# Retention's chunk loop reordered one chunk deeper on four engines

## The chip, the cores and the metric

One of the eight cores of a Trainium2 chip runs the kernel. The metric is the device time of one execution in microseconds (us). Five engines of the core work at once, each through its own list of instructions in order: TensorE (PE in the profile, its weight loads PEld), VectorE (DVE), ScalarE (ACT), GpSimd (POOL) and SyncE (SP), which here only starts DMA transfers. They wait for each other by semaphores.

## The reference

The reference is one layer of a hybrid decoder, for a prompt of 1024 tokens and for 64 new tokens (8 sequences of 8). What the change touches is the retention half of the mixing sub-layer. The prompt is cut into 8 chunks of 128 tokens, and a state S per head is carried from chunk to chunk. Per chunk:

```
inner = einsum('bihd,bjhd->bhij', q, k) * decay[None]
o = (einsum('bhij,bjhe->bihe', inner, v)
     + einsum('bihd,bhde->bihe', q, S) * cross_decay[None, :, :, None])
S_new = S * exp(C * log_g) + einsum('bjhd,bjhe,jh->bhde', k, v, k_decay)
```

Each head's output of 64 values is then normalized and gated:

```
mu = mean(ro); var = mean(square(ro - mu))
ro = (ro - mu) * rsqrt(var + GN_EPS) * g_ret
ro = ro * silu(rg)
```

The new tokens go through the same formula with a state of their own for each sequence. Beside retention the layer has a dilated window attention, an output projection and a SwiGLU feed-forward part.

## The kernel before

The program runs in stages, each a block that every engine enters and leaves together: the input projection (to about 372 us of the span), retention (about 376 to 477), the prompt's attention, the new tokens' attention, and the output projection with the feed-forward part. The change is in the retention block alone. The projection has already rotated, scaled and gated the operands and left them in DRAM; `zr[t]` holds chunk t's q, k, v and gate, 1 MB each, loaded by SP.

Chunk t (0 to 7; `SAMPLE` = 8 stands for the new tokens) takes these steps, each a small function in its engine's part:

- PE `turn(t)` (L845) transposes q and k into `qk_ps`; ACT `evacuate(t)` (L716, L717) copies them to `qT` and `kT`, which have two places each.
- PE `inner(t)` (L856) multiplies them into `in_ps`; DVE `scores(t)` (L741) multiplies that with the mask into `inT`. Both exist once, so `scores(t)` waits for the output of chunk t-1, which reads `inT`, and `inner(t+1)` waits for `scores(t)`.
- PE `update(t)` (L864) computes the chunk's share of the state into `su_ps`; DVE `carry(t+1)` (L759, L761) adds it into `S`, which has two places.
- PE `output(t)` (L873 with the state, L876 with `inT` and v) writes `o_ps`, which has two places.
- DVE `centre(t)` (L774 to L780) sums `o_ps`, takes the mean off and writes `oc`; ACT `square(t)` (L724) squares it; DVE `variance(t)` (L786, L788) sums the squares; POOL `late(t)` raises the variance to the power -0.5 (L692) and scales `oc` into `on` (L696); DVE `finish(t)` (L795) multiplies with the gate into `mixr`, which has two places and which SP stores to DRAM.

`oc` and `on` exist once. The order of the work is the order in which these functions are called on each engine. On DVE a pass of the loop is scores(t), carry(t+1), variance(t-1), finish(t-1), centre(t); on PE inner(t), update(t), turn(t+1), output(t); on ACT evacuate(t+1), square(t); on POOL late(t). In the pass of t = 2 DVE also builds a small table (`build_rows`, L574). After the loop stands the tail for the new tokens: PE multiplies a bias table (`sample_products`, L593), then 64 small products with the loaded states and 16 with `inT` (L894, L897), then the new states (L906); DVE does scores, the last state, a large masked copy `vm` (L645), centre(SAMPLE), the states' sums (L824) and two table copies (L581), with which the block ends.

Of the kernel before, what the change touches and what calls it, by code (L numbers as in the profile page):

```python
# [28 lines left out]
ACT = mybir.ActivationFunctionType  # L29
# [3 lines left out]
HD, NH, NPAIR = 64, 8, 4  # L33
# [7 lines left out]
PT = SEQ // 128  # L41
TT = PT + 1
# [97 lines left out]
def spread(ap, shape):  # L140

    return ap.unsqueeze(2).broadcast_to(shape)
# [385 lines left out]
class DistanceTables:  # L528
# [4 lines left out]
    rows = staticmethod(lambda g: 66 if g == 2 else 99)  # L533
# [26 lines left out]
    def finish(self, sp):  # L560
        sp.wait_ge(self.bias_landed, 16 * NH)
# [37 lines left out]
def retention(nc, A, z, mix, ident, ret, state_p, state_s, tab, bias_p, bias_s, kept_on, stored, ahead):  # L599


    with ExitStack() as ctx:
        sb = lambda n, s, d=F32: ctx.enter_context(nc.sbuf_tensor(n, s, d))
# [7 lines left out]
        inT = sb("inT", [128, 2, NPAIR, 128])  # L611
        S = sb("S", [128, 2, NPAIR, 128])
        kd = sb("kd", [NS, NH, HD])
        oc, sq, on = (sb(n, [128, NH, HD]) for n in ("oc", "sq", "on"))
        stat, mhalf = sb("stat2", [128, TT, 5, NH]), sb("mhalf2", [128, NH])
        mixr, S_out, S_last = kept_on
        S_in = sb("S_in", [128, DEC_B, NPAIR, 128])
# [17 lines left out]
        def head(t, a, h, n=1):  # L635
            return zr[t][0:tile_rows(t), a, h:h + n, :].rearrange("t h d -> t (h d)")
# [11 lines left out]
        with nc.Block() as block:  # L648
# [32 lines left out]
            @block.gpsimd  # L681
            def _(pool):
                pool.memset(mhalf[:, :], -0.5).then_inc(cleared, 1)
                pool.memset(S[:, :, :, :], 0.0).then_inc(cleared, 1)
                pool.memset(qdm[:, :, :], 0.0).then_inc(cleared, 1)
                pool.memset(S_in[:, :, :, :], 0.0).then_inc(cleared, 1)
                pool.wait_ge(cleared, 1)

                def late(t):
                    rows = tile_rows(t)  # L690
                    pool.wait_ge(var_ready, t + 1)
                    pool.tensor_tensor(stat[0:rows, t, 4, :], stat[0:rows, t, 3, :], mhalf[0:rows, :], ALU.pow).then_inc(rstd_ready, 1)  # L692
                    pool.wait_ge(rstd_ready, t + 1)
                    if t:
                        pool.wait_ge(mix_ready, t)
                    pool.tensor_tensor(on[0:rows], oc[0:rows], spread(stat[0:rows, t, 4, :], [rows, NH, HD]),  # L696
                                       ALU.mult).then_inc(on_ready, 1)

                for t in range(PT):
                    late(t)  # L700
                    if t == 3:
                        pool.wait_ge(landed[SAMPLE], 16)
                        pool.tensor_tensor(kd[:, :, :], zr[SAMPLE][0:NS, 1], spread(last_s[:, :], [NS, NH, HD]),
                                           ALU.mult).then_inc(kd_ready, 1)
                    if t == 5:
                        one_sequence(pool, slice(DEC_B // 2 + 1, DEC_B))
                late(SAMPLE)

            @block.scalar
            def _(act):  # L710
                def evacuate(t):
                    rows = tile_rows(t)
                    act.wait_ge(qk_turned, t + 1)
                    if t >= 2:
                        act.wait_ge(o_done, t - 1)
                    act.copy(qT[:, t % 2, :, 0:rows], qk_ps[0][:, :, 0:rows])  # L716
                    act.copy(kT[:, t % 2, :, 0:rows], qk_ps[1][:, :, 0:rows]).then_inc(qkT_ready, 1)  # L717

                def square(t):
                    rows = tile_rows(t)  # L720
                    act.wait_ge(oc_ready, t + 1)
                    if t:
                        act.wait_ge(square_sum_ready, t)
                    act.activation(sq[0:rows], oc[0:rows], ACT.Square).then_inc(sq_ready, 1)  # L724

                evacuate(0)
                for t in range(PT):
                    evacuate(t + 1)
                    square(t)
                square(SAMPLE)  # L730

            @block.vector
            def _(dve):
                def scores(t):
                    rows = tile_rows(t)
                    dve.wait_ge(inner_done, t + 1)
                    if t:
                        dve.wait_ge(o_done, t)
                    own = mask if t < PT else mask_s
                    for r in range(2):  # L740
                        x = dve.tensor_tensor(inT[0:rows, r, :, 0:rows], in_ps[r][0:rows, :, 0:rows],  # L741
                                              own[:, :].unsqueeze(1).broadcast_to([rows, NPAIR, rows]), ALU.mult)
                    x.then_inc(inT_ready, 1)
# [27 lines left out]
                def centre(t):  # L771
                    rows = tile_rows(t)
                    dve.wait_ge(o_done, t + 1)
                    dve.tensor_reduce(stat[0:rows, t, 0, :], o_ps[t % 2][0:rows], AXX, ALU.add).then_inc(sum_ready, 1)  # L774
                    dve.wait_ge(sum_ready, t + 1)
                    dve.tensor_scalar(stat[0:rows, t, 1, :], stat[0:rows, t, 0, :], -1.0 / HD, None, ALU.mult).then_inc(mean_ready, 1)
                    dve.wait_ge(mean_ready, t + 1)
                    if t:
                        dve.wait_ge(on_ready, t)
                    dve.tensor_tensor(oc[0:rows], o_ps[t % 2][0:rows], spread(stat[0:rows, t, 1, :], [rows, NH, HD]),  # L780
                                      ALU.add).then_inc(oc_ready, 1)

                def variance(t):
# [6 lines left out]
                def finish(t):  # L790
                    rows = tile_rows(t)
                    dve.wait_ge(on_ready, t + 1)
                    if t >= 2:
                        dve.wait_ge(mix_stored[t % 2], 16 * (t // 2))
                    dve.tensor_tensor(mixr[0:rows, t % 2, :], on[0:rows].rearrange("p h d -> p (h d)"), head(t, 3, 0, NH),  # L795
                                      ALU.mult).then_inc(mix_ready, 1)

                tables.clear(dve)
                dve.wait_ge(cleared, 2)
                for t in range(PT):  # L800
                    scores(t)
                    if t + 1 < PT:
                        carry(t + 1)
                    if t == 2:
                        tables.build_rows(dve)
                    if t:
                        variance(t - 1)
                        finish(t - 1)
                    centre(t)
                last_state()  # L810
                scores(SAMPLE)
                sample_queries()
                variance(PT - 1)
                one_sequence(dve, slice(0, DEC_B // 2 + 1))
                finish(PT - 1)
                tables.build_samples(dve, 0)
# [20 lines left out]
            def _(pe):  # L837
# [40 lines left out]
                    mm.then_inc(o_done, 1)  # L878

                turn(0)  # L880
                for t in range(PT):
                    inner(t)
                    update(t)
                    turn(t + 1)
                    output(t)
                inner(SAMPLE)
                tables.sample_products(pe, 0)
                pe.wait_ge(state_landed, 32)
                pe.wait_ge(qd_ready, 1)
# [1386 lines left out]
```

## Time and profile before

| | |
|---|---|
| median of three runs (lowest to highest) | 1695.41 us (1694.04 to 1699.86) |
| the profiled execution's own time | 1691.11 us |
| its span, first to last instruction | 1689.5 us |
| PE busy, share of the span | 94% |
| DVE / ACT / POOL busy | 36% / 24% / 23% |
| granted TensorE clock, mean | 0.968 |

The shares are averages over stages with different limits. PE is busy nearly all of the time in the projection and the feed-forward part; in retention it is not, and the granted clock, a share of the full 2.4 GHz, is lower there than elsewhere (a granted clock of 0.50 is 1.2 GHz). The line of clocks in the page has 7 and 8 tenths in the slices from about 422 to 507 us and 9 in nearly all others. So the stage has to be read by itself: which engine waits for which, and what ends each wait.

### The profile page before, as it was taken

To read this page: it belongs to the slowest core of one execution; us is meant where nothing else is said; L and a number is where in the kernel's file an instruction comes from. 1 tells how busy PE (TensorE), PEld (TensorE's weight loads), DVE (VectorE), ACT (ScalarE), POOL (GpSimd) and SP (SyncE) were. 2 spreads that over 40 slices of the span, in tenths; PEclk is the share of its full clock that TensorE was granted. 3 is DMA by queue.
4 is the path that set the end of the run, shared out by engine and by line. 5 is a ranking of instruction groups with operands and counts; after the bars stand their busy time and mean duration, and the time that the engine had idled before them with its cause. 6 is when DMAs were issued, how large, how long until landed. Compare 5 with 4: busy or idle time off the path is not lost.

```text
span 1689.5 us, 23363 instructions
## 1 busy us (share of the span) xinstructions
PE 1581.5 (94%) x9366; PEld 1369.9 (81%) x9366; DVE 609.5 (36%) x977; ACT 405.8 (24%) x720; POOL 384.4 (23%) x459
## 2 busy tenths in 40 slices
PE   7999999988878888879999999999999999999994
PEld 6788888878745556657889999999999999999983
DVE  2233110105666654433552233333323233332355
ACT  4300121211134544442332111211111111111121
POOL 3254300013322223002554111111111111111111
PEclk9999999998779999989999999999999999999997
DMA  6323334119163109954335654545455354653445
GB/s 210 117 72 122 124 124 160 47 67 323 53 208 114 51 13 362 414 215 115 113 94 188 168 141 128 153 111 161 128 144 153 106 168 116 154 149 113 130 113 166
DMA packets 120272, 245.29 MB, mean 145 GB/s; under 512 B 20652, under 2 KB 82364, under 8 KB 115045
## 3 DMA queue, kind: packets, MB, share of 16 engines
q1 hardware_dynamic: 111400, 157.15, 29.6%
q0 software_dynamic: 6976, 71.32, 14.7%
q10 hardware_dynamic: 1824, 15.83, 2.3%
q8 instruction: 49, 0.80, 0.2%
q14 instruction: 23, 0.19, 0.0%
HBM read 214.08 MB, written 106.21 MB: 190 GB/s over the span
## 4 chain that ended last, share of the span: by engine, by line
PE 52%; DVE 1%; DMA 1%; issue 0%; POOL 0%; ACT 0%; DVEq 0%; POOLq 0%
PE y_ps L2126 30%; PE x_ps L2140 7%; PE y_ps L1730 6%; PE m_ps L2140 4%; PE d_ps L2140 4%; DMA own<-x_mid_scratch 1%; PE x_ps L1777 0%; DVE acc L2057 0%; DVE acc L2061 0%; PE m_ps L1724 0%; POOL stat L1936 0%; DVE acc L2045 0%; DVE m_lo L1676 0%; ACT m_hi L1637 0%; PE y_ps L2181 0%
## 5 line engine op out<-in xcount | busy, mean ns | idle before, releaser
L2126 PE MATMUL y_ps<-h_hi,gu_hi 128*128 128x384 f32 (+1 forms) x1056 | 345.9, 328 | 0.0
L2126 PE MATMUL y_ps<-h_hi,gu_lo 128*128 128x384 f32 (+1 forms) x1056 | 345.5, 327 | 0.0
L2126 PE MATMUL y_ps<-h_lo,gu_hi 128*128 128x384 f32 (+1 forms) x1056 | 345.4, 327 | 0.0
L2126 PEld LDWEIGHTS y_ps<-h_hi,gu_hi 128*128 128x128 f32 x1056 | 198.2, 188 | 2.0
L2126 PEld LDWEIGHTS y_ps<-h_lo,gu_hi 128*128 128x128 f32 x1056 | 198.2, 188 | 2.0
L2126 PEld LDWEIGHTS y_ps<-h_hi,gu_lo 128*128 128x128 f32 x1056 | 198.2, 188 | 0.0
L1904 POOL TENSOR_TENSOR f<-silu,f 128x384 fp32r<-128x384 f32 (+1 forms) x66 | 60.6, 918 | 604.5 <-ACT f L1966 422.4
L478 PE MATMUL z_ps<-w_hi,h_hi 128*128 128x512 f32 x488 | 191.3, 392 | 4.3 <-POOL h_lo L331 4.3
L478 PE MATMUL z_ps<-w_lo,h_hi 128*128 128x512 f32 x488 | 190.6, 391 | 0.0
L478 PE MATMUL z_ps<-w_hi,h_lo 128*128 128x512 f32 x488 | 190.4, 390 | 0.0
L2037 DVE TENSOR_TENSOR silu<-silu,y_ps 128x384 f32<-128x384 f32 (+1 forms) x66 | 35.1, 532 | 357.9 <-ACT silu L1963 352.4
L1963 ACT ACTIVATE silu<-y_ps 128x384 f32<-128x384 f32 (+1 forms) x66 | 31.3, 474 | 525.5 <-PE y_ps L2126 525.2
L2140 PE MATMUL x_ps<-wd,f 128*128 128x512 f32 x528 | 128.9, 391 | 0.0
L2140 PEld LDWEIGHTS x_ps<-wd,f 128*128 128x128 f32 x528 | 98.9, 188 | 19.7
L478 PEld LDWEIGHTS z_ps<-w_hi,h_hi 128*128 128x128 f32 x488 | 91.9, 188 | 24.4 <-POOL h_lo L331 4.9
L478 PEld LDWEIGHTS z_ps<-w_hi,h_lo 128*128 128x128 f32 x488 | 92.0, 189 | 19.3
L478 PEld LDWEIGHTS z_ps<-w_lo,h_hi 128*128 128x128 f32 x488 | 92.0, 189 | 19.0
L2045 DVE TENSOR_TENSOR acc<-acc,x_ps 128x512 f32<-128x512 f32 x99 | 68.0, 688 | 52.2 <-PE x_ps L2140 52.2
L403 DVE TENSOR_TENSOR w_lo<-w_raw,w_hi 128x2048 fp32r<-128x2048 f32 x14 | 31.9, 2288 | 140.2 <-ACT w_hi L350 140.2
L2140 PE MATMUL d_ps<-wd,f 128*128 128x512 f32 x264 | 67.5, 391 | 0.0
L2026 DVE TENSOR_TENSOR gu_lo<-raw,gu_hi 128x1024 fp32r<-128x1024 f32 x42 | 51.3, 1223 | 45.1 <-ACT gu_hi L1951 45.1
L2140 PE MATMUL m_ps<-wd,f 128*128 128x512 f32 x264 | 67.4, 391 | 0.0
(236 smaller groups left out, 2238.9 us busy)
## 6 DMA issues: line engine op xcount, KB each, us to landing
ks_sample<-cache_k_win POOLq DMA_DIRECT2D x60, 544.0 KB, 6.5
vs_sample<-cache_v_win POOLq DMA_DIRECT2D x60, 544.0 KB, 7.8
raw<-w_gu SPq DMA_DIRECT2D x84, 256.0 KB, 7.0
K<-cache_k_win SPq DMA_DIRECT2D x8, 2048.0 KB
w_raw<-w_in SPq DMA_DIRECT2D x14, 1024.0 KB
z_scratch<-z_out SPq DMA_DIRECT2D x56, 256.0 KB, 2.0
raw<-w_down SPq DMA_DIRECT2D x22, 512.0 KB, 5.5
zr<-z_scratch SPq DMA_DIRECT2D x8, 1024.0 KB, 10.3
```

What stands on the lines that cost most here:

```text
L403: dve.tensor_tensor(w_lo[cut], w_raw[:, q], w_hi[cut].bitcast(F32), ALU.subtract).then_inc(w_lo_ready, 1)
L478: mm = pe.matmul(z_ps[t % 3][:, :], x[:, k, end - 128:end], w[:, par, k, :], start=(k, n) == first, stop=(k, n) == last)
L1730: mm = pe.matmul(self.y_ps[t % 2][:, c:c + 512], x[:, t % 2, k, :], w, start=(k, n) == (0, 0), stop=(k, n) == (KT - 1, 2))
L1904: low = pool.tensor_tensor(f_lo[cut], f_t[:, 0:n_p], f_hi[cut].bitcast(F32), ALU.subtract)
L1963: act.activation(s_t[:, 0:n], gate_ps[u % 2][:, 0:n], ACT.Silu).then_inc(silu_ready, 1)
L2026: dve.tensor_tensor(lo(p), src(p), hi(p).bitcast(F32), ALU.subtract).then_inc(lo_ready, 1)
L2037: dve.tensor_tensor(f_t[:, 0:n], s_t[:, 0:n], up_ps[u % 2][:, 0:n], ALU.mult).then_inc(f_ready, 1)
L2045: dve.tensor_tensor(acc[cut], acc[cut], d_ps[(2 * (1 - par) + j) % 4], ALU.add).then_inc(added, 1)
L2126: mm = pe.matmul(bank[u % 2][:, 0:n], w[s][:, k, h, :], x[:, k, c:c + n], start=(k, m) == (0, 0), stop=(k, m) == (KT - 1, 2))
L2140: mm = pe.matmul(d_ps[(2 * (1 - par) + j) % 4][:, :], x[:, s, :], w[:, s, col:col + 512], start=(s, m) == (0, 0), stop=(s, m) == (SUB - 1, ...
```

## The change

No instruction is added or taken away; sizes stay. The places of two buffers and the order of the calls change:

- `oc` gets two places. POOL scales in place (`oc` to `oc`), and `on` is gone. `finish` reads `oc`.
- PE now does inner(t+1), output(t), turn(t+2), update(t+1) in a pass, with turn(0), inner(0), turn(1), update(0) ahead of the loop.
- DVE now does scores(t), centre(t-1), carry(t+1), variance(t-1), finish(t-2) in a pass. `centre(t)` waits for finish(t-2) and no longer for POOL's scaling of chunk t-1.
- ACT does evacuate(0) and evacuate(1) first, and evacuate(t+2) ahead of square(t).
- After the loop DVE does scores(SAMPLE) and the new tokens' queries ahead of centre(7) and the last state; finish(6) comes between variance(7) and the masked copy.

```
@@ -611,7 +611,7 @@
         inT = sb("inT", [128, 2, NPAIR, 128])
         S = sb("S", [128, 2, NPAIR, 128])
         kd = sb("kd", [NS, NH, HD])
-        oc, sq, on = (sb(n, [128, NH, HD]) for n in ("oc", "sq", "on"))
+        oc, sq = sb("oc", [128, 2, NH, HD]), sb("sq", [128, NH, HD])
         stat, mhalf = sb("stat2", [128, TT, 5, NH]), sb("mhalf2", [128, NH])
         mixr, S_out, S_last = kept_on
         S_in = sb("S_in", [128, DEC_B, NPAIR, 128])
@@ -691,9 +691,7 @@
                     pool.wait_ge(var_ready, t + 1)
                     pool.tensor_tensor(stat[0:rows, t, 4, :], stat[0:rows, t, 3, :], mhalf[0:rows, :], ALU.pow).then_inc(rstd_ready, 1)
                     pool.wait_ge(rstd_ready, t + 1)
-                    if t:
-                        pool.wait_ge(mix_ready, t)
-                    pool.tensor_tensor(on[0:rows], oc[0:rows], spread(stat[0:rows, t, 4, :], [rows, NH, HD]),
+                    pool.tensor_tensor(oc[0:rows, t % 2], oc[0:rows, t % 2], spread(stat[0:rows, t, 4, :], [rows, NH, HD]),
                                        ALU.mult).then_inc(on_ready, 1)
 
                 for t in range(PT):
@@ -721,11 +719,13 @@
                     act.wait_ge(oc_ready, t + 1)
                     if t:
                         act.wait_ge(square_sum_ready, t)
-                    act.activation(sq[0:rows], oc[0:rows], ACT.Square).then_inc(sq_ready, 1)
+                    act.activation(sq[0:rows], oc[0:rows, t % 2], ACT.Square).then_inc(sq_ready, 1)
 
                 evacuate(0)
+                evacuate(1)
                 for t in range(PT):
-                    evacuate(t + 1)
+                    if t + 2 < TT:
+                        evacuate(t + 2)
                     square(t)
                 square(SAMPLE)
 
@@ -775,9 +775,9 @@
                     dve.wait_ge(sum_ready, t + 1)
                     dve.tensor_scalar(stat[0:rows, t, 1, :], stat[0:rows, t, 0, :], -1.0 / HD, None, ALU.mult).then_inc(mean_ready, 1)
                     dve.wait_ge(mean_ready, t + 1)
-                    if t:
-                        dve.wait_ge(on_ready, t)
-                    dve.tensor_tensor(oc[0:rows], o_ps[t % 2][0:rows], spread(stat[0:rows, t, 1, :], [rows, NH, HD]),
+                    if t >= 2:
+                        dve.wait_ge(mix_ready, t - 1)
+                    dve.tensor_tensor(oc[0:rows, t % 2], o_ps[t % 2][0:rows], spread(stat[0:rows, t, 1, :], [rows, NH, HD]),
                                       ALU.add).then_inc(oc_ready, 1)
 
                 def variance(t):
@@ -792,25 +792,29 @@
                     dve.wait_ge(on_ready, t + 1)
                     if t >= 2:
                         dve.wait_ge(mix_stored[t % 2], 16 * (t // 2))
-                    dve.tensor_tensor(mixr[0:rows, t % 2, :], on[0:rows].rearrange("p h d -> p (h d)"), head(t, 3, 0, NH),
+                    dve.tensor_tensor(mixr[0:rows, t % 2, :], oc[0:rows, t % 2].rearrange("p h d -> p (h d)"), head(t, 3, 0, NH),
                                       ALU.mult).then_inc(mix_ready, 1)
 
                 tables.clear(dve)
                 dve.wait_ge(cleared, 2)
                 for t in range(PT):
                     scores(t)
+                    if t:
+                        centre(t - 1)
                     if t + 1 < PT:
                         carry(t + 1)
                     if t == 2:
                         tables.build_rows(dve)
                     if t:
                         variance(t - 1)
-                        finish(t - 1)
-                    centre(t)
-                last_state()
+                    if t >= 2:
+                        finish(t - 2)
                 scores(SAMPLE)
                 sample_queries()
+                centre(PT - 1)
+                last_state()
                 variance(PT - 1)
+                finish(PT - 2)
                 one_sequence(dve, slice(0, DEC_B // 2 + 1))
                 finish(PT - 1)
                 tables.build_samples(dve, 0)
@@ -878,12 +882,16 @@
                     mm.then_inc(o_done, 1)
 
                 turn(0)
+                inner(0)
+                turn(1)
+                update(0)
                 for t in range(PT):
-                    inner(t)
-                    update(t)
-                    turn(t + 1)
+                    inner(t + 1)
                     output(t)
-                inner(SAMPLE)
+                    if t + 2 < TT:
+                        turn(t + 2)
+                    if t + 1 < PT:
+                        update(t + 1)
                 tables.sample_products(pe, 0)
                 pe.wait_ge(state_landed, 32)
                 pe.wait_ge(qd_ready, 1)
```

DVE in the chunk loop, the change's rows with + and those it replaces with -. `in_ps0` and `in_ps1` are the two halves of the inner products, `zr2` and `zr1` the gates of chunks 2 and 1:

```order
 L786 TENSOR_REDUCE stat2<-sq 128x8
 L788 TENSOR_SCALAR stat2<-stat2 128x8
-L795 TENSOR_TENSOR mixr<-on,zr2 128x512
+L795 TENSOR_TENSOR mixr<-oc,zr1 128x512
+L741 TENSOR_TENSOR inT<-in_ps0,mask 128x512
+L741 TENSOR_TENSOR inT<-in_ps1,mask 128x512
 L774 TENSOR_REDUCE stat2<-o_ps1 128x8
 L776 TENSOR_SCALAR stat2<-stat2 128x8
 L780 TENSOR_TENSOR oc<-o_ps1,stat2 128x512
-L741 TENSOR_TENSOR inT<-in_ps0,mask 128x512
-L741 TENSOR_TENSOR inT<-in_ps1,mask 128x512
 L761 TENSOR_TENSOR S<-S,su_ps 64x4x64 x2
```

Behind the variance of chunk 2 stood the gate of chunk 2, which needs POOL's work on that same variance; now the gate of chunk 1 stands there. The mask products moved from behind the centring to ahead of it.

PE in one pass before, from inner(2) on (the output's eight products come in pairs of four rows, of which two are shown):

```order
L856 MATMUL in_ps<-qT,kT 128x128 x8
L864 MATMUL su_ps<-zr 128x128 x4
L845 MATMUL qk_ps<-ident,zr 128x128 x8
L873 MATMUL o_ps<-S,qT 128x128
L876 MATMUL o_ps<-zr,inT 128x64 x2
```

PE in one pass of the changed kernel, from turn(3) on:

```order
L849 MATMUL qk_ps<-ident,zr 128x128 x8
L868 MATMUL su_ps<-zr 128x128 x4
L860 MATMUL in_ps<-qT,kT 128x128 x8
L877 MATMUL o_ps<-S,qT 128x128
L880 MATMUL o_ps<-zr,inT 128x64 x2
```

Before, a chunk's inner products came first and its output last, with the state's update and the next transposes between. Now the inner products just ahead of an output belong to the next chunk.

## Rows read from the trace of the kernel before

**Rows 1.** Stretch, length; busy PE, PEld, DVE, ACT, POOL; granted clock, DMA, GB/s.

```profile
398.20:407.80 9.60, 9.60 (x52) 9.26 (x52) 5.87 (x18) 0.63 (x1) 2.69 (x2) 0.50 0.80 226
408.30:425.30 17.00, 13.09 (x124) 12.24 (x124) 10.90 (x21) 4.07 (x8) 6.36 (x5) 1.00 0.77 295
386.44:447.94 61.50, 51.20 (x394) 48.45 (x396) 38.36 (x74) 11.05 (x21) 22.50 (x16) 0.82 0.58 190
```

**Rows 2.** Waits, 386.4 to 448 us: waiter, releaser: total, times, longest.

```profile
DVE mixr L795 <- POOL on L696: 20.2, 7, 3.0
```

**Rows 3.** DVE in order of time: start, length, instruction, [idle before, releaser].

```profile
386.47 0.69 DVE L774 TENSOR_REDUCE stat<-o_ps 128x8 f32<-128x512 f32 x1 [2.53 <-PE o_ps L876]
...
403.95 0.69 DVE L774 TENSOR_REDUCE stat<-o_ps 128x8 f32<-128x512 f32 x1
...
405.49 1.28 DVE L741 TENSOR_TENSOR inT<-in_ps,mask 128x512 f32<-128x512 f32 x2
406.68 0.84 DVE L761 TENSOR_TENSOR S<-S,su_ps 64x256 f32<-64x256 f32 x2
...
411.32 0.69 DVE L795 TENSOR_TENSOR mixr<-on,zr 128x512 f32<-128x512 f32 x1 [2.87 <-POOL on L696]
...
447.97 0.69 DVE L774 TENSOR_REDUCE stat<-o_ps 128x8 f32<-128x512 f32 x1 [1.11 <-PE o_ps L876]
```

**Rows 4.** POOL in order of time, the work of chunk 2.

```profile
408.53 1.64 POOL L692 TENSOR_TENSOR stat<-stat,mhalf 128x8 f32<-128x8 f32 x1 [5.34 <-DVE stat L788]
410.24 1.04 POOL L696 TENSOR_TENSOR on<-oc,stat 128x512 f32<-128x512 f32 x1
```

**Rows 5.** PE in order of time, one pass at full clock.

```profile
410.85 1.16 PE L856 MATMUL in_ps<-qT,kT 64*128 64x128 f32 x16
411.94 1.16 PE L864 MATMUL su_ps<-zr 128*128 128x128 f32 x8
412.94 1.04 PE L845 MATMUL qk_ps<-ident,zr 128*128 128x128 f32 x8
414.92 0.49 PE L873 MATMUL o_ps<-S,qT 128*128 128x128 f32 x2 [0.94 <-DVE inT L741]
...
417.74 1.16 PE L856 MATMUL in_ps<-qT,kT 64*128 64x128 f32 x16
```

**Rows 6.** PE, from an output at half clock to the transposes' end.

```profile
397.53 0.49 PE L873 MATMUL o_ps<-S,qT 128*128 128x128 f32 x2 [2.24 <-DVE inT L741]
...
406.16 1.91 PE L845 MATMUL qk_ps<-ident,zr 128*128 128x128 f32 x8
```

**Rows 7.** ACT, the second copy behind those transposes.

```profile
408.59 0.59 ACT L717 COPY kT<-qk_ps 128x512 f32<-128x512 f32 x1
```

**Rows 8.** DVE, the table of the third pass, and a gate beside POOL's work.

```profile
398.91 0.64 DVE L574 TENSOR_TENSOR rel_t<-rel,whose 99x24 f32<-99x24 f32 x6 [0.68 <-DMA whose<-c_whose]
...
419.42 1.51 DVE L795 TENSOR_TENSOR mixr<-on,zr 128x512 f32<-128x512 f32 x1 [2.87 <-POOL on L696]
```

**Rows 9.** POOL: its product that ran beside that gate.

```profile
419.34 1.04 POOL L703 TENSOR_TENSOR kd<-zr,last_s 64x512 f32<-64x512 f32 x1
```

**Rows 10.** DVE: the variance of chunk 7, the masked copy, the tail's centring.

```profile
452.87 0.17 DVE L788 TENSOR_SCALAR stat<-stat 128x8 f32<-128x8 f32 x1
452.95 2.81 DVE L645 TENSOR_TENSOR vm<-zr,bmask 64x2560 f32<-64x2560 f32 x1
...
462.75 0.68 DVE L774 TENSOR_REDUCE stat<-o_ps 64x8 f32<-64x512 f32 x1 [3.04 <-PE o_ps L897]
```

**Rows 11.** POOL, the power of chunk 7's variance, beside that copy.

```profile
453.12 4.14 POOL L692 TENSOR_TENSOR stat<-stat,mhalf 128x8 f32<-128x8 f32 x1 [6.98 <-DVE stat L788]
```

**Rows 12.** PE in the tail: the bias table's products, twice, and the products between.

```profile
448.92 4.75 PE L593 MATMUL table_ps<-dist_s,rel_t 99*128 99x512 f32 x6
453.59 1.96 PE L894 MATMUL o_ps<-S_in,qdm 128*64 128x128 f32 x16
...
466.08 2.85 PE L593 MATMUL table_ps<-dist_s,rel_t 99*128 99x512 f32 x6
```

More of the change, by code:

```diff
@@ L613, in retention @@
         kd = sb("kd", [NS, NH, HD])
-        oc, sq, on = (sb(n, [128, NH, HD]) for n in ("oc", "sq", "on"))
+        oc, sq = sb("oc", [128, 2, NH, HD]), sb("sq", [128, NH, HD])
         stat, mhalf = sb("stat2", [128, TT, 5, NH]), sb("mhalf2", [128, NH])
@@ L693, in late @@
                     pool.wait_ge(rstd_ready, t + 1)
-                    if t:
-                        pool.wait_ge(mix_ready, t)
-                    pool.tensor_tensor(on[0:rows], oc[0:rows], spread(stat[0:rows, t, 4, :], [rows, NH, HD]),
+                    pool.tensor_tensor(oc[0:rows, t % 2], oc[0:rows, t % 2], spread(stat[0:rows, t, 4, :], [rows, NH, HD]),
                                        ALU.mult).then_inc(on_ready, 1)
@@ L723, in square @@
                         act.wait_ge(square_sum_ready, t)
-                    act.activation(sq[0:rows], oc[0:rows], ACT.Square).then_inc(sq_ready, 1)
+                    act.activation(sq[0:rows], oc[0:rows, t % 2], ACT.Square).then_inc(sq_ready, 1)
                 evacuate(0)
+                evacuate(1)
                 for t in range(PT):
-                    evacuate(t + 1)
+                    if t + 2 < TT:
+                        evacuate(t + 2)
                     square(t)
@@ L777, in centre @@
                     dve.wait_ge(mean_ready, t + 1)
-                    if t:
-                        dve.wait_ge(on_ready, t)
-                    dve.tensor_tensor(oc[0:rows], o_ps[t % 2][0:rows], spread(stat[0:rows, t, 1, :], [rows, NH, HD]),
+                    if t >= 2:
+                        dve.wait_ge(mix_ready, t - 1)
+                    dve.tensor_tensor(oc[0:rows, t % 2], o_ps[t % 2][0:rows], spread(stat[0:rows, t, 1, :], [rows, NH, HD]),
                                       ALU.add).then_inc(oc_ready, 1)
@@ L794, in finish @@
                         dve.wait_ge(mix_stored[t % 2], 16 * (t // 2))
-                    dve.tensor_tensor(mixr[0:rows, t % 2, :], on[0:rows].rearrange("p h d -> p (h d)"), head(t, 3, 0, NH),
+                    dve.tensor_tensor(mixr[0:rows, t % 2, :], oc[0:rows, t % 2].rearrange("p h d -> p (h d)"), head(t, 3, 0, NH),
                                       ALU.mult).then_inc(mix_ready, 1)
@@ L801, in _ @@
                     scores(t)
+                    if t:
+                        centre(t - 1)
                     if t + 1 < PT:
@@ L807, in _ @@
                         variance(t - 1)
-                        finish(t - 1)
-                    centre(t)
-                last_state()
+                    if t >= 2:
+                        finish(t - 2)
                 scores(SAMPLE)
                 sample_queries()
+                centre(PT - 1)
+                last_state()
                 variance(PT - 1)
+                finish(PT - 2)
                 one_sequence(dve, slice(0, DEC_B // 2 + 1))
@@ L880, in _ @@
                 turn(0)
+                inner(0)
+                turn(1)
+                update(0)
                 for t in range(PT):
-                    inner(t)
-                    update(t)
-                    turn(t + 1)
+                    inner(t + 1)
                     output(t)
-                inner(SAMPLE)
+                    if t + 2 < TT:
+                        turn(t + 2)
+                    if t + 1 < PT:
+                        update(t + 1)
                 tables.sample_products(pe, 0)
```

## The prediction

> **What bounds the kernel now.** I read the line of granted clocks on the profile's page first, then the busy times of stretches, the waits, and the instructions of single passes in order of time. The whole program is bound by PE, busy 94% of the span. The chunk loop of retention is not. From the end of output(0), where DVE's sum starts at 386.47, to the end of output(7) at 447.97 [rows 3], seven chunks take 61.5 us, 8.79 each. PE is busy in 51.2 of them, so it stands idle for 10.3, and it has 0.82 of its clock [rows 1].
>
> The idle time has one owner. Nothing on DVE can pass `mixr`, and each `mixr` waits nearly 3 us for POOL, 20.2 us in seven times [rows 2]. The circle is: variance on DVE, the power on POOL (1.64), the scaling on POOL (1.04), the gate on DVE, the centring, the mask products, the carry, the next variance [rows 3, 4]. From the centring's start at 403.95 to the end of the next gate (411.32 + 0.69), behind which the next centring stands, is 8.1 us. The mask products, which PE waits for, stand behind the gate in this circle, and so PE waits too, 0.94 us ahead of one output and 2.24 ahead of another [rows 5, 6].
>
> The idle time is paid twice. Behind the 2.24 us the clock falls: 0.50, which is 1.2 GHz, over 398.2 to 407.8, in which PE is busy all the time. Over 408.3 to 425.3, with the idle 0.94 in it, it is 1.00, the 2.4 GHz [rows 1, 5, 6].
>
> **What the change moves, step by step.** No instruction is added, so everything is a matter of what ends last in a pass.
>
> PE's pass at full clock, counted from the end of output(t-1): the transposes start about 0.1 later and take 1.04; ACT's two copies end 1.11 behind them (the transposes end at 406.16 + 1.91 = 408.07, the second copy at 408.59 + 0.59 = 409.18); the hand-over to PE takes about 0.05; inner(t+1) takes 1.09 (410.85 to 411.94); the output takes 2.82 (414.92 to 417.74) [rows 5 to 7]. The sum is 6.21. The update's 1.0 (411.94 to 412.94) [rows 5] lies inside ACT's 1.11 and costs nothing; if the copies were quicker it would be the term in their place. PE is then idle for some 0.2 to 0.3 us in a pass, well under the 0.94 that left the clock at full.
>
> DVE's pass: mask products 1.19 (405.49 to 406.68), centring 1.54 (403.95 to 405.49), carry and variance 1.85 (406.68 to POOL's start at 408.53), gate 0.73: 5.31 [rows 3, 4], 0.9 under PE's. The mask products now start at once behind output(t-1) and end 1.3 into the pass, where inner(t+1) may start only at 2.3, so they no longer hold PE. The carry starts at 2.8, when the update has been done since 2.1. ACT's square fits behind the copies: they end at 2.3, the centring at 2.8.
>
> POOL gets a whole pass for what stood in the circle. It starts with the variance, some 4.6 into the pass, and needs 2.7 plus what the port costs; its result is wanted a pass later, at the same 4.6, so 3.5 us of cover are left. The new wait in the centring (finish(t-2), the reader of the place that is overwritten) is for an instruction one pass earlier on DVE itself: nothing. The stores of the gates stay in their order on SP's queue. The gate of chunk 2 is the first that waits for a store, of chunk 0; it comes in the pass behind output(3), near 387.6 + 3 x 6.3 + 4.6 = 411, the time at which it came before (411.32) [rows 3], so that wait is covered as it was.
>
> The collision that the change makes: the gate of chunk t-2 now stands right behind the variance that releases POOL. Where such a gate met a POOL product that had started 0.08 earlier, it took 1.51 instead of 0.69 [rows 8, 9]. Where DVE went first, in the tail, POOL lost: `vm` starts 0.08 behind the start of the variance's last instruction, POOL's power 0.17 behind `vm`, and the power takes 4.14 and ends 1.5 behind `vm` [rows 10, 11]. The same sequence, variance then a DVE product of two SBUF operands, is what each pass now has. So I take DVE first: POOL loses about 0.6 of its 3.5 us, which costs nothing. The other end is POOL first every time: the gate waits about 1.64, DVE's pass grows to 6.95, and that is 0.74 over PE's.
>
> The Trainium skill ("SBUF — State Buffer", sections "SBUF: two separate sides" and "Who interferes with whom") says that a DVE instruction with two SBUF inputs and a GpSimd instruction that reads SBUF exclude each other for the whole instruction, and that the order of issue decides who waits. Both pairs of rows agree with it. By that rule alone neither order is excluded, so POOL first is a rival below.
>
> The pass of t = 2 has the little table. DVE was held there until 398.91 by the load of `whose`, and needs 0.55 [rows 8]. With output(1) ending near 393.8 DVE comes to it near 397.4 and waits 1.5; variance and gate follow, the next mask products end near 402.3, and PE wants them at about that time. No cost, but without margin: a load 1 us later costs 1 us once.
>
> The start: turn(1), update(0) and inner(1) now stand ahead of output(0). The first two stood there before, the inner products' 1.09 are new: output(0) ends 1.1 later. Seven passes of 6.21 are 43.5 against 61.5: 18.0 less. The loop: 18.0 - 1.1 = 16.9.
>
> The tail: inner(SAMPLE) is now ahead of output(7), and PE goes on with the bias table at once. At 448.92 these products took 4.67 to the next start, at half clock; at 466.08 the same ones took 2.85 [rows 12]. With PE busy to the end the clock should be full, which gains 1.8, and the sum's start moves by 0.95 more as inner(SAMPLE) is gone from its front. The sequences' products take 9.1 (453.59 to 462.7) [rows 10, 12], so PE is ready for the tail's centring 11.95 behind output(7), where it was 14.8. DVE then has, in its order: mask 0.75 and queries 0.35, centring 1.55, last state 1.8, variance 0.9, gate 0.7, `vm` 2.8, POOL's power 1.5 and scaling 1.04 behind it, gate and table copy 1.4: 12.9 with hand-overs. That is 0.95 behind PE: the gain is 14.8 - 12.9 = 1.9. From there to the block's end nothing changes, and the stages behind it start with the block, so they shift as a whole.
>
> The sum is 16.9 + 1.9 = 18.8 us. A hand-over takes 0.04 to 0.07 us (POOL's scaling starts 0.07 behind the power, the gate 0.04 behind the scaling) [rows 3, 4], and each of the seven passes now has four in line of which the sum has one. For the others I take 0.2 a pass, 1.4 in all: 17.4 us. In the profiled execution that makes 1691.11 - 17.4 = 1673.7. That execution is 4.3 under the median of the runs; against the median it is 1695.41 - 17.4 = 1678.0.
>
> **The rivals.**
>
> POOL first. For it: the gap between the two starts in the tail was only 0.17 us [rows 10, 11]. Against it: it is the same sequence, and DVE won. DVE's 6.95 in place of 6.41 would cost 0.54 in each of the six passes that have a gate, about 3 us, and one or two hits on the scaling as well: a gain of 13 to 14, 1682.
>
> The clock falls once. For it: two falls are seen before, and the waits for the table load or for POOL's copies might add up to one. Against it: each fall came behind idle time of a kind that the new order doesn't have. A pass at half clock takes 10.5 (397.53 to 408.07) [rows 6] against 6.2, and it stayed low for some 10 us [rows 1]: 4.3 us, a gain of 13, 1682.
>
> The clock stays low: slower. PE's work is dense in the new order at either clock, and if the dense small products did not bring the clock back, PE would set a pass of 10.5: 7 x 10.5 + 1.1 = 74.6 against 61.5, 13 us slower, 1708. It decides from the fifth of the seven passes on: each at 10.5 takes 4.1 more than one at 6.4, and 17.4 / 4.1 is 4.2. Against it: PE came back to 1.00 by 408.3 out of just such dense work [rows 1].
>
> The gain doesn't reach the end. If something that hangs on no chunk ends last in the block, a load or the next stage's data, the time stays within 2 us of 1695. For it: the block also ends with SP's stores and loads, of which no row is shown here. Against it: the tail's centring waited for PE, 3.04 us [rows 10], and PE for the chunks.
>
> **How the numbers follow.** The forecast has 0.68, with a range of its own from 1673 to 1683; POOL first 0.10, one fall of the clock 0.10, the gain lost 0.07, the low clock 0.05. The first three are faster by more than 0.3% (5 us, about what a measurement of this kernel can tell from no change): 0.88. Lost is the same: 0.07. The low clock is slower: 0.05. The low end of the range is the sum without hand-overs against a run 4 us under the median, 1672; the high end takes in POOL first and one fall together, and some of the runs' spread: 1688.
>
> **What the profile after would show.** Right: the sums of chunks 0 to 7 start 6.2 to 6.5 us apart; no wait of `mixr` for POOL; the longest PE idle in a pass ahead of the inner products, released by ACT's copies, under 0.5 us; granted clock 1.00 over the loop; the power on POOL at some 2.2 us instead of 1.64, and the gate at 0.69. POOL first would show as gates of 2 us and powers of 1.64; a low clock as passes near 10 with PE busy throughout; a lost gain as a new wait at the end of the block. I am wrong in the main step if passes stay over 7.5 us with a full clock.

## The result, and the profile after

The changed kernel takes 1673.79 us (median of four runs, 1669.60 to 1677.27) against 1694.72 for the kernel before on the same chip (1690.75 to 1699.86). The ratio is 0.987, with an interval from 0.9851 to 0.9889: 1.1 to 1.5% faster. The forecast was 1678.0, with a range from 1672 to 1688.

The two profiled executions are only 15.4 us apart, 1691.11 and 1675.72, so I split them at two instructions: the first transposes of retention, and the last copy of the bias table, which ends the block. An output ends, in this table, where PE's next instruction starts.

| us | before | after | difference |
|---|---|---|---|
| program's start to the first transposes | 375.87 | 377.34 | +1.5 |
| first transposes to the end of output(0) on PE | 10.49 | 11.82 | +1.3 |
| end of output(0) to the end of output(7) | 61.51 | 41.84 | -19.7 |
| end of output(7) to the tail's sum on DVE | 14.88 | 12.64 | -2.2 |
| tail's sum to the last table copy | 14.55 | 14.9 | +0.3 |
| the block (the four rows above) | 101.43 | 81.20 | -20.2 |
| last table copy to the span's end | 1212.2 | 1215.6 | +3.4 |

The first and the last row are untouched code. Over the 13 profiles of this study they range from 374.4 to 377.8 and from 1209.7 to 1215.8, so their +1.5 and +3.4 are scatter. The block's 20.2 us stand beside 20.9 between the medians.

The stretch of the loop in after, where [rows 1] has 51.20 us of PE in 61.50 at a clock of 0.82 (length; busy us of PE, its loads, DVE, ACT and POOL; granted clock; DMA share; GB/s):

```profile
390.60:433.80 43.20, 41.05 (x387) 37.10 (x385) 36.77 (x75) 11.13 (x21) 22.56 (x15) 1.00 0.75 236
```

PE went from 83% busy to 95%, at its full 2.4 GHz. (In the page of the kernel before, the clocks of 7 and 8 tenths begin at about 380 us, with the loop, and not at 422.) The waits from the loop's first sum to the last table copy, 390.6 to 458.1 us (engine, line, releaser: us in all, times, longest):

```profile
PE table_ps L593 <- DVE bias_s L581: 4.4, 1, 4.4
...
PEld in_ps L860 <- ACT kT L715: 3.3, 6, 1.0
DVE inT L741 <- PE o_ps L880: 3.0, 4, 1.5
DVE rel_t L574 <- DMA whose<-c_whose: 1.4, 1, 1.4
PE in_ps L860 <- ACT kT L715: 1.3, 5, 0.3
...
DVE mixr L795 <- POOL oc L694: 0.9, 1, 0.9
...
PE in_ps L860 <- DVE inT L741: 0.8, 1, 0.8
...
DVE mixr L795 <- DMA mix_scratch<-mixr: 0.3, 1, 0.3
```

The 20.2 us in seven waits of `mixr` for POOL [rows 2] are gone. The one left, 0.9, is the gate of chunk 7 in the tail. DVE now waits for PE, and PE for ACT's copies, 0.27 us a pass. On PE, the pass with the little table, and then one pass as the others (start, duration):

```profile
401.21 1.05 PE L849 MATMUL qk_ps<-ident,zr 128*128 128x128 f32 x8
...
403.94 1.16 PE L860 MATMUL in_ps<-qT,kT 64*128 64x128 f32 x16 [0.80 <-DVE inT L741]
...
407.76 1.04 PE L849 MATMUL qk_ps<-ident,zr 128*128 128x128 f32 x8
408.64 1.06 PE L868 MATMUL su_ps<-zr 128*128 128x128 f32 x8
409.97 1.16 PE L860 MATMUL in_ps<-qT,kT 64*128 64x128 f32 x16 [0.27 <-ACT kT L715]
411.06 0.49 PE L877 MATMUL o_ps<-S,qT 128*128 128x128 f32 x2
...
413.79 1.04 PE L849 MATMUL qk_ps<-ident,zr 128*128 128x128 f32 x8
```

In the second, from transposes to transposes (407.76 to 413.79), it is 6.03: 2.21 to the inner products, 1.09 to the output, 2.73 to the next transposes. The same stretch on DVE, from the pass with the little table on, and two rows from later passes:

```profile
400.44 0.64 DVE L574 TENSOR_TENSOR rel_t<-rel,whose 99x24 f32<-99x24 f32 x6 [1.42 <-DMA whose<-c_whose]
...
402.51 1.29 DVE L741 TENSOR_TENSOR inT<-in_ps,mask 128x512 f32<-128x512 f32 x2
403.71 0.68 DVE L774 TENSOR_REDUCE stat<-o_ps 128x8 f32<-128x512 f32 x1
404.43 0.70 DVE L776 TENSOR_SCALAR stat<-stat 128x8 f32<-128x8 f32 x1
405.16 0.69 DVE L780 TENSOR_TENSOR oc<-o_ps,stat 128x512 f32<-128x512 f32 x1
...
407.36 0.17 DVE L788 TENSOR_SCALAR stat<-stat 128x8 f32<-128x8 f32 x1
407.44 0.69 DVE L795 TENSOR_TENSOR mixr<-oc,zr 128x512 f32<-128x512 f32 x1
408.16 1.29 DVE L741 TENSOR_TENSOR inT<-in_ps,mask 128x512 f32<-128x512 f32 x2
...
424.93 0.69 DVE L795 TENSOR_TENSOR mixr<-oc,zr 128x512 f32<-128x512 f32 x1 [0.34 <-DMA mix_scratch<-mixr]
...
428.03 2.11 DVE L776 TENSOR_SCALAR stat<-stat 128x8 f32<-128x8 f32 x1
```

And POOL beside it:

```profile
404.06 1.04 POOL L694 TENSOR_TENSOR oc<-oc,stat 128x512 f32<-128x512 f32 x1
407.61 2.01 POOL L692 TENSOR_TENSOR stat<-stat,mhalf 128x8 f32<-128x8 f32 x1 [2.51 <-DVE stat L788]
...
424.66 1.64 POOL L692 TENSOR_TENSOR stat<-stat,mhalf 128x8 f32<-128x8 f32 x1 [2.62 <-DVE stat L788]
...
427.38 2.74 POOL L645 TENSOR_TENSOR vm<-zr,bmask 64x1536 f32<-64x1536 f32 x1
```

The gate goes at 407.44, ahead of the power, and takes 0.69; the power takes 2.01 instead of the 1.64 of [rows 4]. So far this is what was expected. Two things were not: the gate of chunk 4 (424.93) waits 0.34 for a store, and the centring's small TENSOR_SCALAR, 0.17 us alone, takes 0.70 and 2.11 where it meets POOL's scaling (404.06 to 405.10) and `vm` (427.38 to 430.12).

### The profile page after: what moved, and what is told of

The parts are those of the page before. It is cut to its first block, busy times and chain, and to the rows that moved or that the text cites. A ratio compares the mean times of both kernels' runs of the same rounds, so it can differ in the third digit from the quotient of the medians.

```text
span 1674.2 us, 23354 instructions
## 1 busy us (share of the span) xinstructions
PE 1570.5 (94%) x9366; PEld 1359.5 (81%) x9366; DVE 608.8 (36%) x977; ACT 405.9 (24%) x720; POOL 384.3 (23%) x459
## 4 chain that ended last, share of the span: by engine, by line
PE 52%; DVE 1%; DMA 1%; issue 0%; POOL 0%; ACT 0%; DVEq 0%; POOLq 0%
PE y_ps L2134 30%; PE x_ps L2148 7%; PE y_ps L1738 6%; PE m_ps L2148 4%; PE d_ps L2148 4%; DMA own<-x_mid_scratch 1%; PE x_ps L1785 0%; DVE acc L2065 0%; DVE acc L2069 0%; PE m_ps L1732 0%; POOL stat L1944 0%; DVE acc L2053 0%; DVE m_lo L1684 0%; PE y_ps L2189 0%; ACT raw L2008 0%
```

## The experiments

Each ran with a profile. Passes are the distances of DVE's sums (the first of the chunk's centring) of chunks 0 to 7. In after they add up to 43.20 and not to the 41.84 above, because the sum of chunk 0 starts 1.48 behind the end of its output and that of chunk 7 starts 2.84 behind. Times of one run are given as such. The experiments came in three batches, each on its own chip; the kernel before took 1695.92 beside e1 to e4, 1695.13 beside e5 to e8 and 1693.03 beside e9 to e11.

| kernel | block | seven passes | time |
|---|---|---|---|
| before | 101.43 | 8.18 9.30 8.10 8.90 8.11 10.62 8.29 | 1694.72 |
| after | 81.20 | 6.02 7.05 5.65 5.91 6.02 6.03 6.52 | 1673.79 |
| after, again (e8_after) | 85.01 | 6.02 6.78 5.64 5.91 6.03 7.91 7.09 | 1672.76 |
| e1_dve_only | 82.34 | 5.70 7.50 6.23 5.70 5.71 5.70 6.85 | 1674.78 |
| e2_pe_only | 108.98 | 8.19 8.64 9.59 8.91 10.39 10.84 9.43 | 1698.68 (one) |
| e3_gate_same | 100.38 | 8.18 9.47 8.09 8.91 8.09 10.61 7.64 | 1693.04 (one) |
| e4_warm | 101.15 | 8.18 9.16 8.09 8.90 8.10 10.62 8.29 | 1692.85 (one) |
| e5_tail | 77.30 | 6.02 7.17 5.65 5.90 6.03 6.11 6.43 | 1667.88 (one) |
| e6_fold | 82.90 | 6.02 7.82 7.35 7.12 6.03 6.03 4.82 | 1668.58 (one) |
| e7_all | 82.78 | 5.68 5.68 5.68 5.99 5.49 7.71 6.90 | 1671.98 |
| e10_bias | 85.51 | 6.02 8.12 7.36 7.11 6.03 6.02 6.91 | 1678.06 (one) |
| e9_all_bias | 74.42 | 5.68 5.68 5.68 5.68 5.68 5.68 4.83 | 1665.39 |
| e11_keep_order | 76.17 | 6.02 6.02 6.04 6.02 6.03 6.02 4.83 | 1666.27 |

**Which part of the change does it: the gates.** In the changed kernel, only the gate goes back into the pass of its own variance (and finish(6) behind the loop goes):

```
-                    if t >= 2:
-                        finish(t - 2)
+                        finish(t - 1)
```

> The changed kernel with one thing undone: the gate of chunk t-1 stands behind its own variance again, not a pass later; masks are still first. Theory 1: the late gate is what opens the circle; with VectorE waiting 2.9 us for GpSimd in each pass it takes 5.3 + 2.9 = 8.2 us, block 94 to 98. Rival 3: early masks are what counts, since TensorE waits for those alone: passes 6 to 6.6, block 81 to 85.

```profile
DVE mixr L795 <- POOL oc L694: 20.2, 7, 3.0
DVE inT L741 <- PE o_ps L878: 2.2, 1, 2.2
```

The circle is back to the tenth of a us: 20.2 us in seven waits, as in [rows 2], and passes of 8.1 to 10.6. With all of PE's and ACT's new order in place the block is 1.0 shorter than before; 94 to 98 was expected.

**Each half of the change alone.** e1_dve_only is the changed kernel with the order of before on PE and ACT; e2_pe_only is the kernel before with only PE's and ACT's new order (shortened: the conditions on t and the calls ahead of the loop and behind it are left out):

```
e1, in the changed kernel (e2 is the reverse, in the kernel before)
 for t in range(PT):
-    inner(t + 1)
+    inner(t)
+    update(t)
+    turn(t + 1)
     output(t)
-    turn(t + 2)
-    update(t + 1)
...
-    evacuate(t + 2)
+    evacuate(t + 1)
     square(t)
```

> VectorE's and GpSimd's part of the change alone (two places for oc, masks first, gates two chunks late); TensorE and ScalarE keep the old order. Theory 1: the loop was bound by the circle of VectorE and GpSimd, and VectorE's new order alone opens it. TensorE's old order then has inner 1.1, update and transposes 1.8, output 2.7 = 5.6 us a pass, with ScalarE's copies beside the output; VectorE's pass of 5.3 to 5.9 decides; passes 5.6 to 6.1, the block (first transposes to last table copy) 79 to 83 us where the changed kernel has 81.2 and the old one 101.4; the little table of the third pass may cost 2 us once, as VectorE reaches it sooner and waits for its load. Rival 2: the inner products have to come ahead of the output on TensorE, or the masks wait for them: passes 7.5 or more, block over 90.

> TensorE's and ScalarE's part alone (inner products of the next chunk ahead of the output, copies ahead of squares); VectorE and GpSimd keep the old order. Theory 1: passes stay at the circle's 8.1 to 9 us, block 98 to 103. Rival 2: passes under 7.5, block under 92.

e1 has the whole gain: ratio to before 0.9873 [0.9853, 0.9893], as after's. PE's order of before, let loose, makes passes of 5.70, shorter than the 6.03 of the new one, because copies and transposes of the next chunk then stand a whole output ahead of their inner products: the 0.27 that PE waits for ACT's copies in each pass of after is missing in e1's passes of 5.70. In e2's one profile the block grows by 7.5 us, more than the 98 to 103 that was expected. Its waits of DVE, and one pass of its PE:

```profile
DVE mixr L797 <- POOL on L696: 20.2, 7, 3.0
DVE stat L776 <- PE o_ps L878: 8.3, 4, 2.3
```

```profile
407.70 1.28 PE L858 MATMUL in_ps<-qT,kT 64*128 64x128 f32 x16 [2.89 <-DVE inT L743]
408.91 0.80 PE L875 MATMUL o_ps<-S,qT 128*128 128x128 f32 x2
...
414.08 1.71 PE L847 MATMUL qk_ps<-ident,zr 128*128 128x128 f32 x8
```

The wait for POOL is the same 20.2, and PE's work now hangs in the circle too: the inner products wait 2.89 for the mask products, the output behind them runs at half clock (5.17 us), and DVE waits 8.3 us for such outputs.

**Does the low clock cost the old loop anything?** In the kernel before, eight products whose result nobody reads, in PE's idle time ahead of each output from chunk 1 on (shortened: the condition on t is left out):

```
+    for _ in range(8):
+        pe.matmul(tables.ps[:, 0:128], ident, ident, start=True, stop=True)
     output(t)
```

> The old kernel with eight idle products of 128 by 128 (about 1.8 us at full clock) between the transposes and the output of chunks 1 to 7, written to a bank that nothing reads until later: TensorE has less idle time and the clock should stay at full, while the circle of VectorE and GpSimd stays. Theory 1: the clock is the smaller part of the gain: passes at the circle's 8.1, with about 1 us each extra where the table and the masked copy are built, loop 58 to 60 where it was 61.5, block 96 to 99. Rival 4: the low clock was most of the loss: loop under 52, block under 90. If the products only delay the output, passes of 9 or more.

```profile
385.00:446.20 61.20, 55.90 (x506) 53.39 (x506) 38.20 (x75) 10.93 (x21) 22.48 (x16) 0.96 0.60 192
```

```profile
DVE mixr L795 <- POOL on L696: 20.2, 7, 3.0
```

The clock rises from 0.82 to 0.96, and the loop takes 61.34 instead of 61.5; the 58 to 60 that was expected missed. The low clock cost the old loop next to nothing: the circle set it. The passes of 8.90 and 10.62 in both kernels are the circle too. Their gates met POOL products and took, in the kernel before, 1.51 [rows 8] and 3.22 instead of 0.69.

**The port, and the clock in the new loop.** The small TENSOR_SCALAR is taken out: the centring multiplies the sum itself.

```
-    dve.tensor_scalar(stat[...1, :], stat[...0, :], -1.0 / HD, None, ALU.mult)
-    dve.tensor_tensor(oc, o_ps, spread(stat[...1, :]), ALU.add)
+    dve.scalar_tensor_tensor(oc, spread(stat[...0, :]), -1.0 / HD, o_ps, ALU.mult, ALU.add)
```

> The changed kernel with VectorE's small scaling of the sums (128 by 8) folded into the subtraction, as one instruction with the sums in SBUF and the output in PSUM as inputs. Theory P: the small instruction took up to 2.11 us for 0.17 because it takes the port that VectorE shares with GpSimd and waited for GpSimd's product to end; the folded one doesn't take it and stays at 0.69 to 0.8 beside any GpSimd product, the pass with GpSimd's masked copy goes from 6.52 to 6.0 or less, the other passes stay at TensorE's 6.03. Rival Q: any VectorE instruction on SBUF waits for GpSimd's masked copy: the folded one takes over 2 us in that pass, and the pass stays at 6.5.

```profile
427.77 0.69 DVE L778 SCALAR_TENSOR_TENSOR oc<-stat,o_ps 128x512 f32<-128x512 f32 x1
```

The new centring takes 0.69 beside `vm` too (POOL's starts at 427.29 here and takes 2.74; 427.38 in after), and the pass that meets `vm` falls from 6.52 to 4.82, as theory P had it and not rival Q. But three of the other passes missed their 6.03, and the block is 1.7 longer than after's, because of another wait, first on DVE, then on PE, then PE's clock (window, us, busy as above, 0.51 the clock):

```profile
397.26 0.64 DVE L574 TENSOR_TENSOR rel_t<-rel,whose 99x24 f32<-99x24 f32 x6 [2.39 <-DMA whose<-c_whose]
```

```profile
400.76 1.16 PE L858 MATMUL in_ps<-qT,kT 64*128 64x128 f32 x16 [1.55 <-DVE inT L741]
...
406.36 1.92 PE L847 MATMUL qk_ps<-ident,zr 128*128 128x128 f32 x8
```

```profile
402.50:406.40 3.90, 3.90 (x22) 3.90 (x21) 1.63 (x4) 0.09 (x1) 2.63 (x2) 0.51 1.01 204
```

The load was not later here: DVE starts the table 22.81 us behind the first transposes, 23.10 in after. DVE came to it sooner, since the sum of chunk 0 starts 12.24 us behind the first transposes instead of 13.30. PE's idle 1.55 is paid in one pass (7.82), the fall of the clock behind it in the next two (7.35 and 7.12 instead of 6.03).

**The store.** The changed kernel once more:

> The changed kernel itself, run once more beside the others on the same chip. Its block is expected at 80.9 to 81.5 again; the time of the rest of the program moves by some us from execution to execution, and 1674 give or take 4 is expected.

```profile
426.43 1.54 DVE L795 TENSOR_TENSOR mixr<-oc,zr 128x512 f32<-128x512 f32 x1 [1.84 <-DMA mix_scratch<-mixr]
```

The block missed the expected 80.9 to 81.5. The gate of chunk 4 waits 1.84 for the store of chunk 2, then meets POOL's scaling (426.38, 1.04 long) and takes 1.54: a pass of 7.91. In after the same wait was 0.34. PE pays for it:

```profile
429.44 0.68 PE L860 MATMUL in_ps<-qT,kT 64*64 64x64 f32 x16 [1.70 <-DVE inT L741]
```

Behind these 1.70 us PE's clock falls (0.50 over 431.4 to 436.0), and the tail's table products, 2.80 in after, take 4.58. To take the wait away, the loads of the bias table are issued behind the store of chunk 5 on SP's queue, alone (e10) and in e9 and e11 below:

```
-    tables.load_bias(sp)
     for t in range(2, PT):
         store(t)
+        if t == 5:
+            tables.load_bias(sp)
```

> The changed kernel with the move of the bias table's loads alone. Theory S: no gate waits for a store, passes 4 to 7 stay at 6.0 to 6.5, block 80 to 81.5, where the changed kernel's two profiles had 81.2 and 85.0 with waits of 0.34 and 1.84 us. Rival: the waits come from the load of the states, ahead of the first two stores, and stay.

No gate waits for a store in e10, but none does in e6 either, which lacks the edit and where the wait for the table also puts the gates later; so e10 alone does not show that half of the theory. The pair e7 and e9 below, which differ in this edit alone, does. The block missed what was expected: the table came late here (2.48 of wait, its start 24.10 us behind the first transposes), PE stood idle for 1.86, the clock fell, and `vm` met the small TENSOR_SCALAR for 2.50. On the time of this edit alone e10 tells nothing.

**The tail.** Table copies go between the decode states on DVE, and half of the last state store goes to ACT's queue (that part is left out here):

```
     decode_state(1)
+    tables.build_samples(dve, 1)
     decode_state(2)
     finish(SAMPLE)
     decode_state(3)
-    for n in (1, 2):
-        tables.build_samples(dve, n)
+    tables.build_samples(dve, 2)
```

> The changed kernel with the new end of the tail alone (second table copy ahead of the last states, half of the new states' store from ScalarE's queue). If the last 4.3 us of the block are TensorE's table products waiting for VectorE's copy, the stretch from the last centring to the last copy goes from 14.9 to 10.5 to 12; if something else holds the block's end, the next stage still starts some 92.5 us behind the first transposes in place of the copy's end plus half a us.

From the tail's sum to the last copy it is 10.8 instead of 14.9. The next stage begins 78.5 us behind the first transposes instead of 81.7, so 3.2 us reach it; its first products on PE now wait 3.36 for POOL, where they waited 1.10 in after.

**All of it.** e7 puts e1, the tail and the fold together and builds the little table two chunks later; e9 adds e10's edit; e11 is e9 with PE's and ACT's order of the change.

> A version meant to beat both: the run of VectorE's part alone, with the little table built in the pass of chunk 4 (its load has landed by then), the centring's small scaling folded into the subtraction, and a new end of the tail: the second table copy moves ahead of the last states, so TensorE's last table products run beside them, and half of the new states' store goes out from ScalarE's queue. Theory 1: seven passes of 5.6 to 5.8, loop 39.5 to 41, tail from the last centring to the last copy 10.5 to 12 where it was 14.9, block 74 to 77 against 81.2 of the changed kernel, time 5 to 7 us under it. Rival: VectorE's pass is too tight for a late GpSimd and the stores end the block: block over 79.

> The version of everything together, with one more edit: SP issues the eight loads of the bias table behind the store of chunk 5 instead of behind that of chunk 1, so that the gates' stores no longer queue behind them. Theory S: the 2.4 us that a gate waited for the store of chunk 2's gate, and the fall of the clock behind it, are what kept that version's loop at 43.1; without it passes are 5.5 to 5.8 with the clock at 1.00, loop 39.5 to 41, block 73 to 77, time 4 to 8 us under the changed kernel's 1673. Rival: the bias table lands too late or its loads slow the later stores; block over 80.

> The same edits with TensorE's and ScalarE's new order kept (next inner products ahead of the output). Theory 1: ScalarE's copies stand in TensorE's way, passes 6.03, loop 41 to 42.5, the tail 0.9 shorter, block 74 to 77: no difference to the old TensorE order that a time can show, some 1 us at most.

e7 missed: the gate of chunk 4 waited for a store again (on DVE), and the table products that take 2.80 in after then ran at half clock (on PE):

```profile
423.31 1.02 DVE L793 TENSOR_TENSOR mixr<-oc,zr 128x512 f32<-128x512 f32 x1 [2.37 <-DMA mix_scratch<-mixr]
```

```profile
431.47 5.49 PE L593 MATMUL table_ps<-dist_s,rel_t 99*128 99x512 f32 x6
```

In e9 no gate waits for a store, where two gates of e7 wait 2.8 us in all. Its passes are alike, up to the shorter last one, and PE is busy throughout:

```profile
389.00:428.00 39.00, 39.00 (x386) 37.09 (x385) 32.83 (x68) 10.70 (x21) 23.20 (x15) 1.00 0.55 157
```

It takes 1665.39 (six runs, 1662.05 to 1673.63), ratio to before 0.9839 [0.9816, 0.9862]; e11 1666.27, 0.9836 [0.9813, 0.9858]. Both are faster than before. Against the changed kernel their median is some 8 us lower and the block 5 to 7 us shorter, but their intervals overlap after's, which begins at 0.9851, so the times alone don't settle that. Between the two orders on PE the times tell no difference; only the passes do, 5.68 against 6.02.

## Why the prediction was right

**The main step held.** The late gate opens the circle: e3 undoes it and loses the gain, and e1 does DVE's and POOL's part alone and has all of it. So the late gate is needed, and DVE's and POOL's part is enough; whether the late gate would do without the masks first or the second place of `oc` was not run. PE's new order was no help: in e2's one profile it costs 7.5 us of block, and beside the late gates it is 0.3 a pass slower than the old one.

**The terms of the sum.** Start: +1.3 for +1.1. Seven passes: -19.7 for -18.0, and -16.6 with the allowance. Tail: -2.2 for -1.9. The block: -20.2 for -17.4, in one profile; in e8, the same kernel, it is -16.4, so the block of one profile does not tell which of the terms was off. The passes do, since those that wait for no load or store are alike in both. The sums came 5.65 to 7.05 us apart, and not the 6.2 to 6.5 that I gave as the sign. The pass on PE is the term that was mis-sized, 6.03 for 6.21 + 0.2. The row shows where: transposes to inner products 2.21 as summed, inner products 1.09, but 2.73 stands for 2.82 + 0.1, where the 2.82 had already run to the next instruction's start [rows 5]; and the hand-overs beyond ACT's copies that the 0.2 was for don't exist, as only one (0.27, which the sum had) stands in line on PE. The last pass is shorter, 5.15 between the outputs' starts at 423.12 and 428.27, because the sample's transposes and inner products, which stand between them, are smaller.

**DVE first.** Right, with the power at 2.01 for the 2.2 I gave it and the gate at 0.69. DVE's pass of 5.31 was 5.65 (mask products 402.51 to 408.16), and 5.12 without the 0.53 that the small TENSOR_SCALAR of the centring waited; it was counted at 0.17. The trace shows that it waits until POOL's instruction ends: 0.70 beside the scaling, 2.11 beside `vm`. I had weighed the port only for products of two SBUF operands. The Trainium skill ("SBUF — State Buffer", section "Who interferes with whom") says that `tensor_scalar` too can take the shared pair, and that an instruction with one SBUF input outside such modes doesn't contend; the trace agrees with both, the second by e6's centring, which reads PSUM and one SBUF tile and took its 0.69 beside `vm`.

**Wrong: "the idle time is paid twice".** As a reading of the kernel before it fails: e4 gave the clock back and the loop stayed at 61.34 us. A slower PE costs nothing while DVE and POOL's circle ends later. It holds in the new loop, where PE decides: e6 and e10 pay for 1.55 and 1.86 us of idle time and then for two passes at 7.1 to 7.4. The sum was not touched, since it was made from passes.

**Wrong in size: "no cost, without margin".** The table's load did end last: 0.80 of idle PE instead of 0.27 in after, a pass of 6.55 on PE (401.21 to 407.76), 1.55 with a fall of the clock in e6. The rival "the clock falls once" so came true in e6 and e10, by the wait I named, and in e8, the changed kernel itself, by the wait for a store. That after stayed clear of it was in part luck.

**Wrong: "that wait is covered as it was".** I looked at the gate of chunk 2 alone. That one waits for nothing in after. The gate of chunk 4 waits for the store of chunk 2, which SP issues right behind the bias table's loads:

```profile
408.78 4.55 SPq L557 DMA_DIRECT2D bias_p<-tab_scratch  x8
413.80 12.16 SPq L655 DMA_DIRECT2D mix_scratch<-mixr  x3
```

These are three stores, that of chunk 2 first. It takes 11.0 us to land; the median of the stores is 2.5. Before, the longest took 11.1 too, but the gate of chunk 4 came 17.0 us behind that of chunk 2 (411.32 to 428.33); now it comes 11.9 behind (413.08 to 424.93). With the loads moved (e9 against e7, one profile of each) the wait is gone, though the load of `S_in`, the rival cause in e10, stays where it was. Where the wait was 1.84, in e8, POOL is then first at the port, the rival I had at 0.10, for one gate only.

**The tail.** PE was done first and DVE last, as forecast: the tail's sum starts without a wait.

```profile
431.00 2.80 PE L593 MATMUL table_ps<-dist_s,rel_t 99*128 99x512 f32 x6
434.02 1.93 PE L902 MATMUL o_ps<-S_in,qdm 128*64 128x128 f32 x16 [0.22 <-DVE qdm L750]
...
453.74 4.21 PE L593 MATMUL table_ps<-dist_s,rel_t 99*128 99x384 f32 x6 [4.42 <-DVE bias_s L581]
```

```profile
443.64 0.67 DVE L774 TENSOR_REDUCE stat<-o_ps 64x8 f32<-64x512 f32 x1
...
457.98 0.56 DVE L581 COPY bias_s<-table_ps 128x384 f32<-128x384 f32 x1 [4.30 <-PE table_ps L593]
```

The products of 4.75 at half clock [rows 12] take 2.80. What I left as "nothing changes" holds the next gain: PE waits 4.42 for the copy that stands last on DVE, and its products then take 4.21 at half clock. That is what e5 takes out, 4.1 us of this stretch.

**What stays open.** Why DVE gets the little table 22.8 to 24.1 us behind the first transposes, and why the gate of chunk 4 waits 0.34 us in one execution of the changed kernel and 1.84 in another, was not tested by itself. So the block of one profile (81.20 and 85.01 for the same kernel) is known to some 4 us only.

## What to carry to other kernels

Look for the circle first: when an engine waits the same 3 us in every pass for a short instruction that it released itself, move the consumer a pass later, and then ask of every load and store in that loop whether it keeps up with the shorter pass. A low clock on an engine that isn't deciding is a symptom; test it before you price it, and price it anew once that engine decides. Count small instructions against the shared port by what they can take, not by their size: 8 elements a partition waited 2 us.

## What the runs showed of the hardware

A TENSOR_SCALAR of 128x8 on DVE, 0.17 us alone, took 0.70 and 2.11 beside POOL instructions in after and 2.50 in e10. PE's clock fell to 0.51 behind 1.55 us of idle time within dense work in e6, and stayed at 1.00 behind 0.80 in after and 1.22 in e1. The load of `S_in` held SP's queue for 22.55 us of issuing in after (two halves; 22.16 in the kernel before), and the stores that stand behind it start only then:

```profile
383.68 22.55 SPq L662 DMA_DIRECT2D S_in<-state_ret  x2
406.28 2.46 SPq L655 DMA_DIRECT2D mix_scratch<-mixr  x2
```
